# Expert passes of a hybrid backbone: gated values of two steps turned together, downs two steps behind the gate-ups

## The reference, cut to what matters

```python
def swiglu(h, wg, wu, wd):
    return (jax.nn.silu(h @ wg) * (h @ wu)) @ wd

def moe_swiglu(h, w_router, wg, wu, wd):
    logits = (h @ w_router).astype(F32)
    top_val, top_idx = lax.top_k(logits, TOP_K)
    gates = jax.nn.softmax(top_val, axis=-1)
    comb = jnp.sum(jax.nn.one_hot(top_idx, N_EXPERTS, dtype=F32) * gates[..., None], axis=-2)
    out = jnp.zeros(h.shape, F32)
    for e in range(N_EXPERTS):
        out = out + comb[..., e:e + 1] * swiglu(h, wg[e], wu[e], wd[e]).astype(F32)
    return out.astype(h.dtype)
```

## Time and profile before

| | |
|---|---|
| median of three runs | 1684.57 us |
| the profiled execution | 1683.59 us, its span 1681.8 us |
| granted TensorE clock, mean | 0.98 |
| PE busy | 1605.0 us, 95% of the span, 7452 instructions |
| PEld busy | 1270.1 us, 76% |
| DVE busy | 1290.1 us, 77% |
| ACT busy | 898.7 us, 53% |
| POOL busy | 40.7 us, 2% |
| from HBM | 401.03 MB, 239 GB/s over the span |
| chain that ended last | PE 75%, DVE 16%, ACT 5%, issue 2%, DMA 2% |

### The profile page before, as it was taken

The page is one execution under the profiler, slowest core; times in us unless marked ns, Lnnn a source line. Parts: engine busy times, 40 slices in busy tenths (PEclk is TensorE's granted clock), DMA queues, the critical chain, the costliest instruction groups (busy, mean ns, idle before and its releaser), DMA issues.

```text
span 1681.8 us, 19520 instructions
## 1 busy us (share of the span) xinstructions
PE 1605.0 (95%) x7452; PEld 1270.1 (76%) x7452; DVE 1290.1 (77%) x1723; ACT 898.7 (53%) x1029; POOL 40.7 (2%) x40
## 2 busy tenths in 40 slices
PE   5999999899999999999889999999999999999996
PEld 2785567778888888786587788888888888888875
DVE  2944474698787765765668999898989999898997
ACT  3324363322222222445657777777777777777764
POOL 1000000000000000000000000000000000000050
PEclk8999999899999999999989999999999999999999
DMA  9225510363445554232057998899999999999983
GB/s 391 89 76 191 219 63 31 129 243 129 175 171 210 201 194 150 74 122 94 17 201 277 353 368 343 345 360 365 360 346 348 359 356 347 359 357 358 375 330 118
DMA packets 55971, 403.43 MB, mean 240 GB/s; under 512 B 6416, under 2 KB 6448, under 8 KB 8768
## 3 DMA queue, kind: packets, MB, share of 16 engines
q1 hardware_dynamic: 53712, 387.47, 61.0%
q0 software_dynamic: 2160, 14.63, 2.4%
HBM read 401.03 MB, written 1.05 MB: 239 GB/s over the span
## 4 chain that ended last, share of the span: by engine, by line
PE 75%; DVE 16%; ACT 5%; issue 2%; DMA 2%; SPq 0%; DVEq 0%; ACTq 0%
PE PS L449 20%; PE PS L451 20%; PE PS L450 20%; DVE w_lo L2273 6%; DVE w_lo L1634 2%; PE PS L754 2%; DMA arena<-in_ada 2%; ACT w_hi L1506 1%; DVE arena L1647 1%; PE PS L1009 1%; PE PS L779 1%; PE PS L766 1%; PE PS L733 1%; DVE XT L2000 1%; PE PS L459 1%
## 5 line engine op out<-in xcount | busy, mean ns | idle before, releaser
L2273 DVE TENSOR_TENSOR w_lo<-arena,w_hi 128x2048 fp32r<-128x2048 f32 (+1 forms) x136 | 306.0, 2255 | 40.4 <-ACT w_hi L1506 37.6
L2273 DVE TENSOR_TENSOR w_lo<-raw,w_hi 128x2048 fp32r<-128x2048 f32 (+1 forms) x133 | 299.0, 2252 | 29.9 <-ACT w_hi L1506 26.8
L1506 ACT CAST w_hi<-arena 128x2048 fp32r<-128x2048 f32 x132 | 252.4, 1915 | 43.1 <-PE PS L451 42.6
L1506 ACT CAST w_hi<-raw 128x2048 fp32r<-128x2048 f32 x129 | 246.8, 1916 | 40.6 <-PE PS L451 40.3
L449 PE MATMUL PS<-hT_hi,w_hi 128*128 128x512 f32 (+1 forms) x576 | 216.0, 375 | 8.3 <-DVE hT_lo L1780 6.6
L450 PE MATMUL PS<-hT_lo,w_hi 128*128 128x512 f32 (+1 forms) x576 | 213.7, 371 | 0.0
L451 PE MATMUL PS<-hT_hi,w_lo 128*128 128x512 f32 (+1 forms) x576 | 213.4, 371 | 0.0
L449 PE MATMUL PS<-w_hi,hT_hi 128*128 128x512 f32 (+1 forms) x448 | 178.7, 399 | 1.1 <-DVE w_lo L1634 0.6
L451 PE MATMUL PS<-w_hi,hT_lo 128*128 128x512 f32 (+1 forms) x448 | 174.3, 389 | 0.0
L450 PE MATMUL PS<-w_lo,hT_hi 128*128 128x512 f32 (+1 forms) x448 | 173.6, 387 | 0.0
L1634 DVE TENSOR_TENSOR w_lo<-raw,w_hi 128x2048 fp32r<-128x2048 f32 (+1 forms) x54 | 122.4, 2266 | 24.1 <-ACT w_hi L1128 23.9
(11 more groups left out here) (322 smaller groups left out, 2537.1 us busy)
## 6 DMA issues: line engine op xcount, KB each, us to landing
raw<-in_moe SPq DMA_DIRECT2D x132, 1024.0 KB, 6.3
arena<-in_moe SPq DMA_DIRECT2D x132, 1024.0 KB, 6.4
raw<-in_ffn SPq DMA_DIRECT2D x33, 1024.0 KB, 4.9
raw<-in_dot SPq DMA_DIRECT2D x28, 1024.0 KB, 4.8
raw<-in_ada SPq DMA_DIRECT2D x17, 1024.0 KB, 6.7
raw<-in_out SPq DMA_DIRECT2D x8, 1024.0 KB, 4.8
raw<-in_inb SPq DMA_DIRECT2D x8, 960.0 KB, 4.8
raw<-in_ina SPq DMA_DIRECT2D x5, 1024.0 KB, 4.9
```

Of the source, the lines that this page charges most:

```text
L1506: nc.scalar.copy(w_hi[:, x_slot(j), :], x_raw(n)).then_inc(x_hi, 1)
L2273: last = v.tensor_tensor(w_lo[:, x_slot(j), q], x_raw(NGR * (i % 2) + j)[:, q], w_hi[:, x_slot(j), q].bitcast(F32), ALU.subtract)
```

## The change

It has three parts, in the expert passes alone; the dense layer keeps its order.

1. The turns take two steps at once. `turn_h(t)` transposes the four blocks of steps 2t and 2t + 1 into the 512 columns of bank 2, behind the first gate-up half of an even step; a pass has six turns (TURNS), the last with step 10's two blocks alone. The cast `high_turned` and the subtraction `low_turned` take 512 columns each, the last 256.
2. The downs run two steps behind the gate-ups: behind the gate-ups of step s comes the down of step s - 2, and at the end of the pass, behind down 8, the last turn, down 9 and down 10. The granules arrive in that order (`pass_order`, also in `lay`).
3. ACT and DVE split each granule three places ahead of PE's: in step s the granules three behind ("gu", s, 0) and ("gu", s, 1), then Silu and the gated product, then the granule three behind ("d", s - 2, 0). In the last step both engines take the granule three behind ("gu", 10, 1) after Silu and product, and the halved subtraction there goes.

```diff
+TURNS = (FC + 1) // 2
...
+def pass_order():
+
+    order = []
+    for s in range(FC):
+        order += [("gu", s, 0), ("gu", s, 1)]
+        if s > 1:
+            order.append(("d", s - 2, 0))
+    return order + [("d", FC - 2, 0), ("d", FC - 1, 0)]
...
-        fpos = {x: i for i, x in enumerate(order)}
+        fpos = {x: i for i, x in enumerate(pass_order())}
...
+        def turns_to(s):
+
+            return (FC + 1) // 2 if s == FC - 1 else s // 2 + 1
+
+        def turned(n):
+
+            return PS[:, 2, 0:256 * n].rearrange("p (s c) -> p s c", c=256)
+
+        def steps_of(t):
+
+            return range(2 * t, min(2 * t + 2, FC))
...
-                def turn_h(s):
-                    eng.wait_ge(x_h, FC * i + s + 1)
-                    if i or s:
-                        eng.wait_ge(x_tlo, FC * i + s)
-                    for f in range(2):
-                        last = nc.tensor.transpose(PS[:, 2, P * f:P * f + P], hh[:, s % 2, P * f:P * f + P],
-                                                   ident[:, :])
+                def turn_h(t):
+                    eng.wait_ge(x_h, FC * i + steps_of(t)[-1] + 1)
+                    if i or t:
+                        eng.wait_ge(x_tlo, TURNS * i + t)
+                    for s in steps_of(t):
+                        for f in range(2):
+                            a = 256 * (s % 2) + P * f
+                            last = nc.tensor.transpose(PS[:, 2, a:a + P], hh[:, s % 2, P * f:P * f + P], ident[:, :])
                     last.then_inc(x_turned, 1)
...
                     gate_up(s, 0)
-                    if s:
-                        turn_h(s - 1)
+                    if s and s % 2 == 0:
+                        turn_h(s // 2 - 1)
                     if s == 0:
                         eng.wait_ge(x_glo, 4 * m + 4)
                     gate_up(s, 1)
-                    if s == FC - 1:
-                        down(s - 1, (0,))
-                        turn_h(s)
-                        down(s - 1, (1,))
-                    elif s:
-                        down(s - 1)
+                    if s > 1:
+                        down(s - 2)
...
+                turn_h(TURNS - 1)
+                down(FC - 2)
                 down(FC - 1)
...
-                def high_turned(s):
-                    eng.wait_ge(x_turned, FC * i + s + 1)
-                    if i or s > 1:
-                        j = fpos[("d", s - 2, 0)] + 1 if s > 1 else 0
-                        eng.wait_ge(x_used, NGR * i + j)
-                    nc.scalar.copy(f_hi[:, s % 2, :], PS[:, 2, 0:256]).then_inc(x_thi, 1)
+                def high_turned(t):
+                    eng.wait_ge(x_turned, TURNS * i + t + 1)
+                    n = len(steps_of(t))
+                    if i or t:
+                        eng.wait_ge(x_used, NGR * i + (fpos[("d", 2 * t - 3 + n, 0)] + 1 if t else 0))
+                    nc.scalar.copy(f_hi[:, 0:n, :], turned(n)).then_inc(x_thi, 1)
...
-                    if s:
-                        high_turned(s - 1)
+                    if s and s % 2 == 0:
+                        high_turned(s // 2 - 1)
+                    high(i, fpos[("gu", s, 0)] + RING)
                     if s + 1 < FC:
-                        for j in range(fpos[("gu", s + 1, 0)] if s else RING, fpos[("gu", s + 1, 1)] + 1):
-                            high(i, j)
-                    else:
-                        high(i, fpos[("d", s, 0)])
+                        high(i, fpos[("gu", s, 1)] + RING)
                     eng.wait_ge(x_used, NGR * i + fpos[("gu", s, 1)] + 1)
                     act(sg[:, s % 2, :], PS[:, s % 2, 0:256], ACT.Silu).then_inc(x_silu, 1)
-                    if s + 1 < FC:
-                        high(i, fpos[("d", s, 0)])
-                    else:
-                        high_turned(s)
+                    if s + 1 == FC:
+                        high(i, fpos[("gu", s, 1)] + RING)
+                        high_turned(TURNS - 1)
                         if i + 1 not in LAST:
                             high(i + 1, 0)
+                    elif s > 1:
+                        high(i, fpos[("d", s - 2, 0)] + RING)
...
-                    if s:
-                        low_turned(s - 1)
+                    if s and s % 2 == 0:
+                        low_turned(s // 2 - 1)
+                    low(i, fpos[("gu", s, 0)] + RING)
                     if s + 1 < FC:
-                        for j in range(fpos[("gu", s + 1, 0)] if s else RING, fpos[("gu", s + 1, 1)] + 1):
-                            low(i, j)
-                    else:
-                        low(i, fpos[("d", s, 0)], (0,))
+                        low(i, fpos[("gu", s, 1)] + RING)
                     eng.wait_ge(x_silu, FC * i + s + 1)
                     v.tensor_tensor(hh[:, s % 2, :], PS[:, s % 2, 256:512], sg[:, s % 2, :],
                                     ALU.mult).then_inc(x_h, 1)
-                    low(i, fpos[("d", s, 0)], (0, 1) if s + 1 < FC else (1,))
+                    if s + 1 == FC:
+                        low(i, fpos[("gu", s, 1)] + RING)
+                    elif s > 1:
+                        low(i, fpos[("d", s - 2, 0)] + RING)
```

More of the change, by code:

```diff
@@ L1002, in gate_up, with down @@
                     last.then_inc(x_used, 1)
-                def turn_h(s):
-                    eng.wait_ge(x_h, FC * i + s + 1)
-                    if i or s:
-                        eng.wait_ge(x_tlo, FC * i + s)
-                    for f in range(2):
-                        last = nc.tensor.transpose(PS[:, 2, P * f:P * f + P], hh[:, s % 2, P * f:P * f + P],
-                                                   ident[:, :])
+                def turn_h(t):
[6 more added lines that the diff above has]
+                            last = nc.tensor.transpose(PS[:, 2, a:a + P], hh[:, s % 2, P * f:P * f + P], ident[:, :])
                     last.then_inc(x_turned, 1)
-                def down(s, fs=(0, 1)):
+                def down(s):
                     j = fpos[("d", s, 0)]
                     hi, lo = granule_of(j)
-                    eng.wait_ge(x_tlo, FC * i + s + 1)
+                    eng.wait_ge(x_tlo, TURNS * i + turns_to(s))
                     if s == 0 and i:
                         eng.wait_ge(x_y, 2 * i)
-                    for f in fs:
+                    for f in range(2):
                         a = slice(P * f, P * f + P)
@@ L1024, in down @@
                                           s == 0 and f == 0, s == FC - 1 and f == 1)
-                    if fs[-1]:
-                        last.then_inc(x_used, 1)
+                    last.then_inc(x_used, 1)
                 m = i // 2
@@ L2268, in add_late, with low, low_turned @@
                 last.then_inc(x_late, 1)
-            def low(i, j, halves=(0, 1)):
+            def low(i, j):
                 eng.wait_ge(x_hi, NGR * i + j + 1)
[L2272 to L2276, removed]
+                v.tensor_tensor(w_lo[:, x_slot(j), :], x_raw(NGR * (i % 2) + j), w_hi[:, x_slot(j), :].bitcast(F32),
+                                ALU.subtract).then_inc(x_lo, 1)
             def expert_pass(i):
-                def low_turned(s):
-                    eng.wait_ge(x_thi, FC * i + s + 1)
-                    v.tensor_tensor(f_lo[:, s % 2, :], PS[:, 2, 0:256], f_hi[:, s % 2, :].bitcast(F32),
+                def low_turned(t):
+                    eng.wait_ge(x_thi, TURNS * i + t + 1)
+                    n = len(steps_of(t))
+                    v.tensor_tensor(f_lo[:, 0:n, :], turned(n), f_hi[:, 0:n, :].bitcast(F32),
                                     ALU.subtract).then_inc(x_tlo, 1)
@@ L2310, in expert_pass @@
                         plan_passes(s)
-                low_turned(FC - 1)
+                low_turned(TURNS - 1)
                 if i + 1 not in LAST:
@@ L2509, in swiglu @@
         d5 = wd.reshape(n, FC, 2, P, D)
-        for i, (kind, s, half) in enumerate(ffn_order()):
+        for i, (kind, s, half) in enumerate(pass_order()):
             if kind == "gu":
```

## The result

The changed kernel takes 1698.23 us (median of four runs, 1696.89 to 1699.71), the kernel before beside it 1684.30 us. The ratio is 1.0087, with a 95% interval of 1.0075 to 1.0099: slower by 13.9 us. The profiled execution had 1697.86 us (span 1696.0), against 1683.59 (span 1681.8) before. The predicted time was 1704.6 us with a range of 1693 to 1711; direction and mechanism held, and the size was too large by 6.4 us.

A forecast was written before the change was run, and what follows sets the result against it. The passes were taken as bound by PE's own queue in mid pass. Waits, boundaries and pass 0 (14.7 - 4.0 + 0.9 = +11.6) plus 8.5 for the clock gave +20.1 us, hence 1704.6 us, range 1693 to 1711.

The forecast's parts named there:

- part 3: Step 2's turn waits for step 1's product, 2.10 us in each of passes 1 to 7: +14.7 us.
- part 5: Pass 0: PE waits 3.3 us at the first turn, 4.3 us lost against 3.4 today; +0.9 us entered.
- part 4: Boundary of two passes: small waits of 0.57 us go at seven boundaries, -4.0 us.
- part 1: Fewer, larger turns: four transposes cost what two times two cost, so 0 entered, with -3.6 us as bound.
- part 2: Casts and subtractions of 512 columns: nothing on PE's path in mid pass, 0.5 us of cover left.
- part 6: Pass 7, where GpSimd's sums make DVE the slower engine: 0 entered, between -1 and +2 us.
- part 7: Granted clock falls behind the new waits: four in seven passes, one in pass 0, 1.7 us each, +8.5 us.
- no falls of the clock: Rival: the wait is there but the clock stays up, 1696.2 us; no or few falls had chance 0.24.
- Eight falls: Rival: every wait brings the clock down, +13.6 us, 1709.8 us; chance 0.10.
- failing cover: Rival: mid-pass cover is less than read, PE waits 0.2 us in each of 40 turns, 1712.6 us; chance 0.06.
- The faster rival: Step 2's turn finds its values there, without a wait: 1677.2 us; chance 0.06.

The follow-up runs named there:

- e1: The changed kernel with step 1's Silu and gated product put ahead of the cast and subtraction of the granule three ahead: 1676.50 us, ratio 0.9964 to the kernel before.
- e3: The kernel before with step 1's gated product put behind the subtraction of that step's down granule on VectorE: 1705.26 us, ratio 1.0135.
- e2: e1 with eleven turns of two transposes, casts and subtractions of 256 columns, product early in steps 0 and 1: 1677.35 us, ratio 0.9967 to the kernel before.
- e4: e1 with Silu and gated product ahead of that cast and subtraction in every step: 1675.51 us, ratio 0.9958 to the kernel before.

## Why the prediction was right, point by point

- **The new wait (part 3), right to 0.01 us.** Predicted 2.10 us in passes 1 to 7, measured 2.11. The chain 0.20 + 1.95 + 2.21 + 0.42 + 0.05, put together from single rows of another place in the kernel, against one granule of cover was all that it took. e1 shows that it is the loss, e3 that it is one by itself.
- **Pass 0 (part 5), right.** Predicted a wait of 3.3 us and +0.9 in all; measured 3.28 and +0.60.
- **The boundary (part 4), right.** The two small waits of PE there are gone from the view of waits. Seven times 0.57 us were entered, and e2, which has this gain with neither the new wait nor merged turns, is 0.69 and 0.54 us below the kernel before in passes 1 and 2.
- **Fewer turns (part 1), the term that was missized.** I entered 0 for the merged turns, with -3.6 us as the bound, since four transposes cost 0.44 us and two cost 0.22. That counted a turn only up to the second matmul behind it. From turn to turn two steps take 16.80 us after the change (16.78 in e1) and 16.87 with pairs of turns, 0.06 to 0.09 us less for each of 40 pairs, or some 2.5 us in all by the 0.31 us of pass 2. Without the four falls the difference of all passes is 14.9 - 4 x 1.6 = 8.5 us, where the parts 1 to 6 gave 11.6. Of these 3.1 us the merge in passes 0 to 6 is 7 x 0.31 = 2.2, and pass 7 has 0.7. The estimate of -3.6 us by the Trainium skill's figure (TensorE: Matmul & The Clock Gate, "Wait - 56ns, not 53.3ns?"), which I had set aside, lies nearer than 0, though not for its own reason: the transposes do start 0.11 us apart and not 0.056, and the saving is in the matmuls behind a turn.
- **Larger casts (part 2), right.** No wait in mid pass; e4, which moves casts and subtractions by some 0.3 us, leaves the passes as they are. That the small instructions of an odd pass stand ahead of the larger subtraction was not in the prediction; it costs 0.28 us in e1, and nothing in the changed kernel, whose first turn comes later.
- **Pass 7 (part 6), within its bounds.** It grew by 0.85 us; the wait less the boundary would be 1.5, so 0.7 came back. e4 shows DVE as the bound there, and e2, with single turns, takes 0.8 us more than e1. The prediction had worked out a change of 0.15 us in DVE's work per two steps and entered 0 for it; five times 0.15 would be the 0.7. That this is the cause was not tried by itself.
- **The clock (part 7), the price right, the criterion wrong.** Five falls of 1.7 us were entered, 8.5 us; there were four of 1.6 (pass 5 against pass 3, 101.94 - 100.33), 6.4 us. The length of the gap was to decide. But the one that I was surest of, behind the longest wait, 3.3 us in pass 0, didn't come: the window 897 to 905 us has 1.00. That four of the seven others came, as entered, is luck: I had no rule for them but that 2.33 us lay near an edge.

```profile
897.00:905.00 8.00, 5.09 (x25) 4.30 (x26) 6.89 (x14) 4.13 (x4) 0.00 (x0) 1.00 0.80 297
```

  The edge itself was read from one execution. The gap of 2.61 us of the earlier trace rows is in code that the change doesn't touch, and in the profile of the changed kernel the same gap has no fall behind it:

```profile
370.98 0.50 PE L472 MATMUL PS<-h_hi,w_hi 128*128 128x512 f32 x1 [2.22 <-DVE XT L2020]
...
372.00:380.00 8.00, 7.27 (x32) 5.66 (x31) 7.79 (x17) 1.24 (x2) 0.00 (x0) 1.00 0.41 147
```

  Of the eight profiled executions of this study only two, those of the kernel before and of e2, have a fall at this gap.

- **The rest.** The first pass began at 882.99 us instead of 883.99, in code that the change doesn't touch; in the eight profiled executions it began between 881.80 and 885.03. 20.1 - 2.1 (clock) - 3.1 (turns and pass 7) = 14.9 us, the difference of the passes. With the 1.0, and 0.3 us more behind the last pass, it is 14.2, the difference of the two spans. The 13.9 us of the medians has the noise of the other executions in it.

The rivals: no falls of the clock (1696.2 us) was 2 us from the measured time and is refuted only by the windows, since the missing fall costs and the missed gain of the turns nearly cancel; a total alone would have chosen it for a wrong reason. The rule that the prediction quotes beside it excepts the gap of pass 0, which with one fall of 1.7 us would make it 1697.9 us, nearer still; but the trace has falls behind four of the short gaps and none behind that one. Eight falls and a failing cover didn't occur. The faster rival named what it would take, a product that isn't behind the cast and the subtraction, and e1 does just that: 1676.5 us, with 1677.2 worked out for it. That the two agree so well is luck in part: the 3.4 us that pass 0 was to give back didn't come (98.67 us in e1, 98.81 before), and the gain of the merged turns and of pass 7, not counted in it, stands in their place.

## What to carry to other kernels

When work is merged over two steps, ask for the first pair, not for the steady one: in mid pass the product had 0.6 us to spare, and in step 2, where no down had begun yet, it was 2.1 us late in seven passes and 3.3 in the first. In an engine's queue, put the short instruction that another engine waits for (here 0.4 us of Silu and 0.4 of product) ahead of the long one that has time; that turned a loss of 14 us into a gain of 6 to 9. A kernel that keeps TensorE busy throughout pays for a wait of 2 us in full, and at times once more in clock.

## What the runs showed of the hardware that was not expected

- A wait of 2.11 us of PE in a dense stretch was followed by a fall of the granted clock in four of seven cases, in each of the two profiled executions of the changed kernel; the one of 3.28 us was followed by none in either. In e3 it was four of seven, and none behind a wait of 1.9 us. The size of a single gap does not decide it. The Trainium skill (TensorE: Matmul & The Clock Gate, "HAM oscillation — how this bites in real kernels") has the clock fall after longer gaps; the rows here have it fall behind 2.1 us.
- The same gap of 2.6 us, in code that all kernels share, had a fall behind it in two of eight executions. A fall seen once behind a gap is no property of that gap.
- The two executions of the changed kernel had their falls in the same four passes; what picks them is open.
- Where the clock fell, it cost 1.6 us, and nothing of that came back later.
- What a group of transposes costs is not all in the starts right behind it: by those, four transposes cost as much as two times two (0.44 us each way), and by the time from turn to turn 0.06 to 0.09 us less.
